# Summing over the second expert table: the high and low inputs pass as one 512-column product

## The chip, the cores and the metric

The kernel runs on one core of a Trainium2 chip. The metric is the device time of one execution, in microseconds: the median of three runs, 2018.12 us, the lowest 2017.0 and the highest 2022.48. In what follows PE is the tensor engine's stream of products, PEld its weight loads, ACT the scalar engine, DVE the vector engine, SP the queue that issues the transfers.

## The reference

The reference is two transformer stages over 256 tokens with 1024 features. The part that the change touches is the expert layer `peer_ffn` of the first stage. Each token scores 16,384 experts by two sets of 128 keys, keeps 16 experts for each of 8 heads, and sums rows of the table `v`, weighted by a gated activation:

```python
def peer_ffn(h, w_q, sub_keys, u, v):
    ...
    def chunk(args):
        hc, ic, gc = args
        a = jnp.einsum('cd,ced->ce', hc, u[ic])
        a = jax.nn.gelu(a, approximate=False) * gc.astype(hc.dtype)
        return jnp.einsum('ce,ced->cd', a, v[ic])
```

Inputs, tables and result are float32.

## The kernel before

The kernel doesn't gather experts. It computes the activation of all 16,384 experts for all 256 tokens, multiplies by the token's weight of each expert (zero for those not chosen), and sums densely over the table `v`. That last sum is the function `expert_sum`: for each of 128 keys j, the 128 experts of that key are the contraction, `arena` holds their weighted activations (128 experts x 256 tokens), and the row block of `v` is 128 experts x 1024 features. The result is 8 feature blocks c of 128 features x 256 tokens, which stay in the accumulation banks over all 128 keys and are added to the residual `x` at the end.

Each float32 operand is split in two of the format fp32r: a high part (rounded) and a low part (what is left). `three` (L509) makes one block product of three: high weights by high input (L512), high weights by low input (L514), low weights by high input (L515). There is one weight load for each product. In `expert_sum` the stationary operand is the table's block and the moving one is the 256 tokens, so a key costs 8 x 3 products of 256 columns.

The work is staged so:

- SP sends one key's 1024 x 128 weights (512 KB) into one of four places of `ring`; a place is free when its low parts are made (`send`, L415).
- ACT makes the high part of half a key's weights, 128 x 512 (`split_high`, L462), once PE has used the half four before it; DVE makes the low part (`split_low`, L468), and PE waits for that before each half. Three halves are prepared ahead (AHEAD). In the same turn of the code ACT makes the high part of a key's input (L2447) and DVE its low part (L2467), two keys ahead.
- A turn of the loop is four keys. The first turn is written out, and 31 more run in a hardware loop. A half is four feature blocks: 12 products of PE, 96 in a turn.
- `next_order` (L517) counts the block products. For most it changes nothing. For a few it hands the 256 columns of one of the three products (L514) in another order: in runs of 16 columns (RUN), taken in turn from each half of the 256 (`parts_at` says 2) or from each quarter (4). The input is read and the bank written in the same order, so the sum is the same. In the loop of this stage it is one of 32 block products per turn; in the written-out first turn it is the fourth, the seventh and the twentieth. Other stages count on in the same way.
- Feature blocks c and c + 1 share a bank of 512 columns, four banks in all, and the first product in a bank clears it.
- After the last half DVE adds the four banks to `x` (L2486), 128 x 512 at a time. The block of code ends there, all engines meet, and the next stage starts: ACT makes the high part of the normed residual (L1059), DVE the low part (L1161), and PE multiplies.

Other places of the program, the wide ones, swap the roles: there 512 columns of weights pass over a stationary 128-token block (the same lines L512, L514, L515, with 128x512 in the form).

Of the kernel before, what the change touches and what calls it, by code (L numbers as in the profile page):

```python
# [23 lines left out]
F32R = mybir.dt.float32r  # L24
BF16 = mybir.dt.bfloat16
ALU = mybir.AluOpType
# [3 lines left out]
P = 128  # L30
T = 256
TT = T // P
D = 1024
DC = D // P
# [6 lines left out]
HALF = 4  # L41
SLOTS = 4
RUN = 16
SIDES = 4
# [11 lines left out]
N_KEYS = 128  # L56
# [241 lines left out]
class Kernel:  # L298
# [1673 lines left out]
    def peer(self):  # L1972

        with self.room(N_KEYS * T):
            with self.pairs(DC):
                self.peer_scores()

            with self.nc.sbuf_tensor("hot", [P, 2, 4, 4, P], F32) as hot:
                self.expert_weights(hot)
            with self.nc.sbuf_tensor("s_high", [P, SIDES, T], F32R) as s_high, \  # L1980
                    self.nc.sbuf_tensor("s_low", [P, SIDES, T], F32R) as s_low:
                self.expert_sum(s_high, s_low)

    def peer_scores(self):

# [407 lines left out]
        for s in (apart, left, right, crossed, merged):  # L2393
            s.total += T // batch

    def expert_sum(self, s_high, s_low):

        nc = self.nc
        first = 2 * (PEER_AT + N_KEYS)
        halves = 2 * RING  # L2400
        turns = N_KEYS // RING
        v = self.dram["peer_v"]
        assert self.split == first + AHEAD
        start = self.sent
        assert start == PEER_AT + N_KEYS + AHEAD // 2 + RING
        cut = self.counter("input_high"), self.counter("input_low")
        with nc.Block(no_gpsimd_drain=True) as block:
            @block.sync
            def _(sp):
                with sp.Fori(0, turns - 2) as it:  # L2410
                    for k in range(RING):
                        g = start + k
                        self.send(sp, g, g % RING, v[it * RING + (g - PEER_AT - N_KEYS)], it, RING)
                self.sent += (turns - 2) * RING
                self.stream(sp, first + 2 * N_KEYS + AHEAD)

            @block.tensor
            def _(pe):
                def turn(it):
                    self.threes = 0 if isinstance(it, int) else 7  # L2420
                    for k in range(RING):
                        pe.wait_ge(cut[1].sem, it * RING + cut[1].at(k + 1))
                        for i in range(2):
                            h = first + 2 * k + i
                            pe.wait_ge(self.low, it * halves + (h + 1))
                            for n in range(HALF):
                                c = HALF * i + n
                                s = slice(n * P, (n + 1) * P)

                                to = self.bank[c // 2][:, (c % 2) * T:(c % 2 + 1) * T]  # L2430
                                opens = isinstance(it, int) and k == 0 and c % 2 == 0
                                ins = self.three(to, ((self.w_high[:, h % SLOTS, s],
                                                       self.w_low[:, h % SLOTS, s]),
                                                      (s_high[:, k % SIDES, :], s_low[:, k % SIDES, :])),
                                                 opens, False, skip_group_check=True)
                            ins.then_inc(self.used, 1)
                turn(0)
                with pe.Fori(1, turns) as it:
                    turn(it)

            @block.scalar
            def _(act):
                def side(k, it):


                    act.wait_ge(self.used, it * halves + (first + 2 * (k - SIDES + 1)))
                    nc.scalar.activation(s_high[:, k % SIDES, :],  # L2447
                                         self.arena[:, bass.ds(it * (RING * T) + k * T, T)],
                                         ACT.Copy).then_inc(cut[0].sem, 1)

                def turn(it, last=False):
                    for k in range(RING):
                        for i in range(2):
                            self.split_high(act, first + AHEAD + 2 * k + i, it, halves)
                        if not last or k < RING - 2:
                            side(k + 2, it)
                side(0, 0)
                side(1, 0)
                with act.Fori(0, turns - 1) as it:
                    turn(it)  # L2460
                turn(turns - 1, True)

            @block.vector
            def _(dve):
                def side(k, it):
                    dve.wait_ge(cut[0].sem, it * RING + cut[0].at(k + 1))
                    nc.vector.tensor_tensor(s_low[:, k % SIDES, :],  # L2467
                                            self.arena[:, bass.ds(it * (RING * T) + k * T, T)],
                                            s_high[:, k % SIDES, :].bitcast(F32), ALU.subtract)\
                        .then_inc(cut[1].sem, 1)  # L2470

                def turn(it, last=False):
                    for k in range(RING):
                        for i in range(2):
                            self.split_low(dve, first + AHEAD + 2 * k + i, it, halves)
                        if not last or k < RING - 2:
                            side(k + 2, it)
                side(0, 0)
                side(1, 0)
                with dve.Fori(0, turns - 1) as it:  # L2480
                    turn(it)
                turn(turns - 1, True)
                dve.wait_ge(self.used, first + 2 * N_KEYS)
                for b in range(DC // 2):
                    part = self.x[:, 2 * b:2 * b + 2, :]
                    nc.vector.tensor_tensor(part, part, self.bank[b][:, :].rearrange(  # L2486
                        "p (c t) -> p c t", c=2), ALU.add)
        for c in cut:
            c.total += N_KEYS
        self.split += 2 * N_KEYS  # L2490
        self.taken += N_KEYS * BLK
# [1037 lines left out]
```

## Time and profile before

| | us |
|---|---|
| median of 3 runs | 2018.12 |
| the profiled execution's own time | 2018.9 |
| its span, first to last instruction | 2017.1 |
| PE busy in the span | 1867.6 (93%) |
| the stage `expert_sum` on PE, first to last product | 829.86 to 1180.41 |
| mean granted clock of PE over the span | 0.975 |

A busy PE says little about its pace, since products overlap: the record of a 256-column product lasts 0.28 us while a new one starts every 0.11 us. The pace is read from the starts of consecutive products. A start is shown to 0.01 us, so the pace is taken over a long run without gaps. The granted clock is 1.00 at 2.4 GHz and 0.50 at 1.2 GHz.

### The profile page before, as it was taken

The page shows a single profiled execution, that of the slowest core. Times are in us where ns is not written, and L with a number is a line of the kernel's source. Part 1 is how long each engine was busy: PE and PEld are TensorE (multiplying, and loading weights), DVE is VectorE, ACT ScalarE, POOL GpSimd, SP SyncE. Part 2 cuts the span into 40 slices and gives each one's busy share as a digit, 9 for nine tenths or more (in the row PEclk, how much of TensorE's full clock was granted, in tenths as well). Part 3 has the DMA queues.
Part 4 walks back from the last instruction along what each step waited for, and adds up shares of the span by engine and source line. Part 5 has one row for each costly group of instructions (what it writes and reads, how often), then busy time and mean ns, then how long its engine had stood idle before and what let it go on. Part 6 is the DMA issues. An engine that isn't in the chain of part 4 may idle for free. (4 is left out here: it accounts for less than half of the span.)

```text
span 2017.1 us, 45016 instructions
## 1 busy us (share of the span) xinstructions
PE 1867.6 (93%) x16518; PEld 1789.4 (89%) x16518; DVE 1454.4 (72%) x3046; ACT 1237.5 (61%) x2420; POOL 0.2 (0%) x4
## 2 busy tenths in 40 slices
PE   8998988999999989999999989687999977899996
PEld 7887888999999976899999989587999976899996
DVE  7667566788986479766666667776787687578857
ACT  5455655777777789655555555733665564666545
POOL 0000000000000000000000000000000000000000
PEclk9999999999999999999999999798999999999998
DMA  6533344466565620266666646101665644166562
GB/s 205 161 98 105 116 146 127 137 196 188 185 184 175 195 83 0 88 194 192 193 192 193 192 141 194 58 3 49 189 197 172 187 136 136 32 185 197 180 194 77
DMA packets 102084, 296.06 MB, mean 147 GB/s; under 512 B 9539, under 2 KB 32454, under 8 KB 101830
## 3 DMA queue, kind: packets, MB, share of 16 engines
q1 hardware_dynamic: 101958, 294.35, 47.5%
q8 instruction: 83, 1.36, 0.3%
q14 instruction: 43, 0.35, 0.1%
HBM read 293.26 MB, written 1.05 MB: 146 GB/s over the span
## 5 line engine op out<-in xcount | busy, mean ns | idle before, releaser
L468 DVE TENSOR_TENSOR w_low<-ring,w_high 128x512 fp32r<-128x512 f32 x1102 | 742.3, 684 | 354.6 <-ACT w_high L462 348.0
L512 PE MATMUL bank<-a_high,w_high 128*128 128x256 f32 x3228 | 917.2, 284 | 78.3 <-DVE w_low L468 42.9
L514 PE MATMUL bank<-a_low,w_high 128*128 128x256 f32 x3228 | 904.8, 280 | 0.0
L515 PE MATMUL bank<-a_high,w_low 128*128 128x256 f32 x3228 | 904.0, 280 | 0.0
L462 ACT ACTIVATE w_high<-ring 128x512 fp32r<-128x512 f32 x1102 | 666.1, 623 | 347.3 <-PE bank L515 345.4
L512 PEld LDWEIGHTS bank<-a_high,w_high 128*128 128x128 f32 x3228 | 616.6, 191 | 95.0 <-DVE w_low L468 44.1
L514 PEld LDWEIGHTS bank<-a_low,w_high 128*128 128x128 f32 x3228 | 616.4, 191 | 0.4
L515 PEld LDWEIGHTS bank<-a_high,w_low 128*128 128x128 f32 x3228 | 616.0, 191 | 0.0
L512 PE MATMUL bank<-s_high,w_high 128*128 128x256 f32 x1024 | 283.6, 277 | 2.0 <-DVE s_low L2467 2.0
L514 PE MATMUL bank<-s_low,w_high 128*128 128x256 f32 x1024 | 283.7, 277 | 0.0
L515 PE MATMUL bank<-s_high,w_low 128*128 128x256 f32 x1024 | 283.6, 277 | 0.0
L512 PEld LDWEIGHTS bank<-s_high,w_high 128*128 128x128 f32 x1024 | 193.1, 189 | 2.2 <-DVE s_low L2467 2.2
L515 PEld LDWEIGHTS bank<-s_high,w_low 128*128 128x128 f32 x1024 | 193.0, 189 | 0.0
L514 PEld LDWEIGHTS bank<-s_low,w_high 128*128 128x128 f32 x1024 | 192.9, 188 | 0.0
L2349 PEld LDWEIGHTS bank<-hot 128*128 128x128 f32 x512 | 61.9, 191 | 29.2 <-issue 18.9
L2093 ACT ACTIVATE arena<-bank 128x256 f32 (+1 forms) x128 | 49.2, 384 | 56.2 <-PE bank L515 55.7
L2349 PE MATMUL bank<-hot 128*128 128x128 f32 x512 | 73.6, 287 | 10.0 <-ACT hot L2286 8.9
L1059 ACT ACTIVATE a_high<-x,params 128x256 fp32r<-128x256 f32 x72 | 32.0, 500 | 49.3 <-DVE x L1292 34.8
L1066 ACT ACTIVATE a_high<-arena 128x256 fp32r<-128x256 f32 x87 | 30.5, 407 | 42.3 <-DVE arena L1352 24.9
L2467 DVE TENSOR_TENSOR s_low<-arena,s_high 128x256 fp32r<-128x256 f32 x128 | 53.4, 418 | 0.8 <-ACT s_high L2447 0.8
L2320 DVE TENSOR_SCALAR hot<-consts,hn 128x128 f32<-128x128 f32 x192 | 53.2, 341 | 0.4 <-PEq L2042 0.4
L2447 ACT ACTIVATE s_high<-arena 128x256 fp32r (+1 forms) x128 | 51.5, 403 | 2.7 <-PEq L2263 2.7
(368 smaller groups left out, 1862.8 us busy)
## 6 DMA issues: line engine op xcount, KB each, us to landing
ring<-in_stream SPq DMA_DIRECT2D x273, 512.0 KB, 3.6
ring<-in_peer_u SPq DMA_DIRECT2D x128, 512.0 KB, 3.6
ring<-in_peer_v SPq DMA_DIRECT2D x128, 512.0 KB, 3.5
ring<-in_stream SPq DMA_DIRECT2D x32, 256.0 KB, 3.2
ring<-in_stream SPq DMA_DIRECT2D x12, 192.0 KB, 2.8
x<-in_x SPq DMA_DIRECT2D x4, 256.0 KB, 6.6
arena<-in_mem SPq DMA_DIRECT2D x1, 1024.0 KB, 11.4
out<-x SPq DMA_DIRECT2D x4, 256.0 KB, 2.6
```

Source lines behind the costliest of these rows:

```text
L462: self.nc.scalar.activation(self.cut(h, self.w_high), self.raw(h), ACT.Copy)\
L468: self.nc.vector.tensor_tensor(self.cut(h, self.w_low), self.raw(h), self.cut(h, self.w_high.bitcast(F32)), ALU.subtract)\
L512: self.nc.tensor.matmul(to, lh, rh, start=start, stop=False, **more)
L514: self.nc.tensor.matmul(order(to), lh, order(rl), start=False, stop=False, **more)
L515: return self.nc.tensor.matmul(to, ll, rh, start=False, stop=stop, **more)
L1059: ins = nc.scalar.activation(self.a_high[:, to, :], source.source[:, c, :], ACT.Copy, scale=self.param(source.gain, c))
L1066: ins = nc.scalar.activation(self.a_high[:, to, :], source[:, c, :], ACT.Copy)
L2093: nc.scalar.activation(to, self.bank[k % 4][:, 0:T], ACT.Gelu)\
L2320: ins = nc.vector.tensor_scalar(hot[:, 1, b, i, :], iota, one(1), one(2), ALU.is_equal, ALU.mult)
L2349: ins = nc.tensor.matmul(self.bank[b][:, i * P:(i + 1) * P], hot[:, 0, b, i, :], hot[:, 1, b, i, :], start=True, stop=True)
L2447: nc.scalar.activation(s_high[:, k % SIDES, :], self.arena[:, bass.ds(it * (RING * T) + k * T, T)], ACT.Copy).then_inc(cut[0].sem, 1)
L2467: nc.vector.tensor_tensor(s_low[:, k % SIDES, :], self.arena[:, bass.ds(it * (RING * T) + k * T, T)], s_high[:, k % SIDES, :].bitcast(F32) ...
```

## The change

In `expert_sum` the high and low part of a key's input now lie side by side in one buffer, `s_both`, with two lots of 256 columns. A block product is two products of PE: the high weights pass over all 512 columns at once (L2431), and the low weights over the 256 columns of the high part (L2435). A feature block then needs a bank of its own: its first 256 columns collect high x high and low x high, its last 256 columns high x low. All eight banks are used. The other order of columns goes to the product of the low weights, one in each turn of the loop as before. At the end DVE adds both halves of each bank to `x`: 16 additions of 128 x 256, in four groups of four, with a wait on its own chain between the two groups that write the same `x`, and a first wait that asks only for the first four feature blocks.

```diff
-            with self.nc.sbuf_tensor("s_high", [P, SIDES, T], F32R) as s_high, \
-                    self.nc.sbuf_tensor("s_low", [P, SIDES, T], F32R) as s_low:
-                self.expert_sum(s_high, s_low)
+            with self.nc.sbuf_tensor("s_both", [P, SIDES, 2, T], F32R) as s_both:
+                self.expert_sum(s_both)
...
+        s_high, s_low = s_both[:, :, 0, :], s_both[:, :, 1, :]
...
-                                to = self.bank[c // 2][:, (c % 2) * T:(c % 2 + 1) * T]
-                                opens = isinstance(it, int) and k == 0 and c % 2 == 0
-                                ins = self.three(to, ((self.w_high[:, h % SLOTS, s],
-                                                       self.w_low[:, h % SLOTS, s]),
-                                                      (s_high[:, k % SIDES, :], s_low[:, k % SIDES, :])),
-                                                 opens, False, skip_group_check=True)
+                                opens = isinstance(it, int) and k == 0
+                                nc.tensor.matmul(self.bank[c][:, :], self.w_high[:, h % SLOTS, s],
+                                                 s_both[:, k % SIDES, :, :], start=opens, stop=False,
+                                                 skip_group_check=True)
+                                order = self.next_order(self.bank[c][:, 0:T])
+                                ins = nc.tensor.matmul(order(self.bank[c][:, 0:T]),
+                                                       self.w_low[:, h % SLOTS, s],
+                                                       order(s_high[:, k % SIDES, :]), start=False,
+                                                       stop=False, skip_group_check=True)
...
-                dve.wait_ge(self.used, first + 2 * N_KEYS)
-                for b in range(DC // 2):
-                    part = self.x[:, 2 * b:2 * b + 2, :]
-                    nc.vector.tensor_tensor(part, part, self.bank[b][:, :].rearrange(
-                        "p (c t) -> p c t", c=2), ALU.add)
+                link = self.chain(dve, "dve")
+                for i in range(2):
+                    dve.wait_ge(self.used, first + 2 * N_KEYS - 1 + i)
+                    for part in range(2):
+                        for c in range(HALF * i, HALF * i + HALF):
+                            ins = nc.vector.tensor_tensor(
+                                self.x[:, c, :], self.x[:, c, :],
+                                self.bank[c][:, part * T:(part + 1) * T], ALU.add)
+                        if part == 0:
+                            link(ins)
```

On PE, the half of the loop's turn that holds the other order of columns stands so before (`128x8x2x16` is that order; banks 2 and 3 hold feature blocks 4 to 7):

```order
L512 MATMUL bank2<-s_high,w_high 128x256
L514 MATMUL bank2<-s_low,w_high 128x8x2x16
L515 MATMUL bank2<-s_high,w_low 128x256
L512 MATMUL bank2<-s_high,w_high 128x256
L514 MATMUL bank2<-s_low,w_high 128x256
L515 MATMUL bank2<-s_high,w_low 128x256
L512 MATMUL bank3<-s_high,w_high 128x256
L514 MATMUL bank3<-s_low,w_high 128x256
L515 MATMUL bank3<-s_high,w_low 128x256
```

The same half on PE with the change:

```order
L2431 MATMUL bank4<-s_both,w_high 128x512
L2435 MATMUL bank4<-s_both,w_low 128x8x2x16
L2431 MATMUL bank5<-s_both,w_high 128x512
L2435 MATMUL bank5<-s_both,w_low 128x256
L2431 MATMUL bank6<-s_both,w_high 128x512
L2435 MATMUL bank6<-s_both,w_low 128x256
L2431 MATMUL bank7<-s_both,w_high 128x512
L2435 MATMUL bank7<-s_both,w_low 128x256
```

Twelve products of 256 columns become four of 512 and four of 256: the columns are the same 3072 in a half, the weight loads are 8 where they were 12.

On DVE, the end of the stage before:

```order
L468 TENSOR_TENSOR w_low<-ring,w_high 128x512 x2
L2467 TENSOR_TENSOR s_low<-arena,s_high 128x256
L468 TENSOR_TENSOR w_low<-ring,w_high 128x512 x2
L2467 TENSOR_TENSOR s_low<-arena,s_high 128x256
L468 TENSOR_TENSOR w_low<-ring,w_high 128x512 x4
L2486 TENSOR_TENSOR x<-x,bank 128x512 x4
```

and with the change:

```order
L468 TENSOR_TENSOR w_low<-ring,w_high 128x512 x2
L2470 TENSOR_TENSOR s_both<-arena,s_both 128x256
L468 TENSOR_TENSOR w_low<-ring,w_high 128x512 x2
L2470 TENSOR_TENSOR s_both<-arena,s_both 128x256
L468 TENSOR_TENSOR w_low<-ring,w_high 128x512 x4
L2491 TENSOR_TENSOR x<-x,bank 128x256 x16
```

The additions stand behind the last low parts of weights in both, and only they differ. On ACT and SP the order of the work is the same as before.

## Rows read from the trace of the kernel before

**Rows 1.** The page: busy time of each engine in the whole span.

```profile
PE 1867.6 (93%) x16518; PEld 1789.4 (89%) x16518; DVE 1454.4 (72%) x3046; ACT 1237.5 (61%) x2420; POOL 0.2 (0%) x4
```

**Rows 2.** Windows of the stage: us, busy us (records) per engine, granted clock, DMA share, GB/s.

```profile
831.00:835.00 4.00, 4.00 (x24) 4.00 (x23) 1.07 (x3) 1.57 (x3) 0.00 (x0) 0.57 0.45 133
840.00:1180.00 340.00, 340.00 (x2997) 340.00 (x2996) 213.99 (x374) 195.79 (x373) 0.00 (x0) 1.00 0.62 193
```

**Rows 3.** Waits between 820 and 1200 us: who waited for whom, us in total, times, longest.

```profile
ACT w_high L462 <- PE bank L515: 153.9, 259, 1.6
DVE w_low L468 <- ACT w_high L462: 131.2, 255, 1.5
PE bank L512 <- DVE a_low L1161: 4.0, 1, 4.0
PE bank L512 <- DVE s_low L2467: 2.0, 1, 2.0
```

**Rows 4.** Timeline of PE in the stage, three places: start us, us, engine, line.

```profile
834.64 0.28 PE L512 MATMUL bank<-s_high,w_high 128*128 128x256 f32 x1
...
838.29 0.28 PE L514 MATMUL bank<-s_low,w_high 128*128 128x256 f32 x1
...
838.88 0.28 PE L512 MATMUL bank<-s_high,w_high 128*128 128x256 f32 x1
...
901.20 0.28 PE L512 MATMUL bank<-s_high,w_high 128*128 128x256 f32 x1
901.32 0.28 PE L514 MATMUL bank<-s_low,w_high 128*128 128x256 f32 x1
...
901.79 0.28 PE L515 MATMUL bank<-s_high,w_low 128*128 128x256 f32 x1
...
902.58 0.28 PE L512 MATMUL bank<-s_high,w_high 128*128 128x256 f32 x1
...
911.76 0.28 PE L512 MATMUL bank<-s_high,w_high 128*128 128x256 f32 x1
```

**Rows 5.** Timeline of PE in a later stage, first and last of 78 products.

```profile
1912.90 0.28 PE L512 MATMUL bank<-a_high,w_high 128*128 128x256 f32 x1
...
1921.97 0.28 PE L515 MATMUL bank<-a_high,w_low 128*128 128x256 f32 x1
```

**Rows 6.** Timeline of PE: 512-column products in fp32r, then 256-column ones.

```profile
1256.92 0.39 PE L514 MATMUL bank<-w_low,a_high 128*128 128x512 f32 x1
...
1263.10 0.39 PE L514 MATMUL bank<-w_low,a_high 128*128 128x512 f32 x1
...
1268.50 0.28 PE L512 MATMUL bank<-a_high,w_high 128*128 128x256 f32 x1
...
1269.20 0.28 PE L512 MATMUL bank<-a_high,w_high 128*128 128x256 f32 x1
```

**Rows 7.** Timeline of PE: two 512-column products in bf16.

```profile
823.81 0.38 PE L2355 MATMUL bank<-hn,small 128*128 128x512 bf16 x1
824.03 0.38 PE L2358 MATMUL bank<-hn 128*128 128x512 bf16 x1
```

**Rows 8.** Timeline of all engines at the end of the stage.

```profile
1180.09 0.69 DVE L468 TENSOR_TENSOR w_low<-ring,w_high 128x512 fp32r<-128x512 f32 x1 [0.67 <-ACT w_high L462]
...
1180.41 0.28 PE L515 MATMUL bank<-s_high,w_low 128*128 128x256 f32 x1
1180.72 2.48 DVE L2486 TENSOR_TENSOR x<-x,bank 128x512 f32<-128x512 f32 x4
1183.55 3.30 ACT L1059 ACTIVATE a_high<-x,params 128x256 fp32r<-128x256 f32 x8 [3.50 <-PEq L2407]
```

**Rows 9.** Timeline of DVE in a later stage: 256-column additions from a bank.

```profile
1343.53 1.40 DVE L2996 TENSOR_TENSOR arena<-arena,bank 128x256 f32<-128x256 f32 x4
```

**Rows 10.** Windows behind the stage, columns as in rows 2.

```profile
1180.00:1182.00 2.00, 0.69 (x7) 0.49 (x5) 1.91 (x4) 0.05 (x1) 0.00 (x0) 1.00 0.76 225
1183.00:1189.00 6.00, 4.28 (x20) 4.31 (x21) 3.48 (x9) 5.45 (x14) 0.00 (x0) 0.50 0.01 3
1190.00:1194.00 4.00, 1.55 (x14) 1.35 (x13) 2.12 (x3) 3.93 (x6) 0.00 (x0) 1.00 0.00 0
```

More of the change, by code:

```diff
@@ L2394, in expert_weights, with expert_sum @@
             s.total += T // batch
-    def expert_sum(self, s_high, s_low):
+    def expert_sum(self, s_both):
+        s_high, s_low = s_both[:, :, 0, :], s_both[:, :, 1, :]
         nc = self.nc
```

## The prediction

> **What bounds the kernel now.** I read the page first: PE is busy 93% of the span, far ahead of DVE (72%) and ACT (61%) [rows 1]. That is an average, so I went to the stage that the change touches. Between 840 and 1180 us PE is busy every microsecond, at the full clock, while DVE works 214 of 340 us, ACT 196, and the transfers take 62% [rows 2]. The waits say the same: ACT waits 153.9 us for PE to give weight slots back, DVE 131.2 us for ACT, and PE waits once for 2.0 us at the stage's start and once for 4.0 us behind its end [rows 3]. So the stage lasts as long as PE's stream of products does, and what counts is the time from the start of one product to the next. That is read from the timeline, not from the busy time.
>
> Three paces of fp32r products can be read there:
> - 256 columns, most of the stage: 81 steps from 902.58 to 911.76, 9.18 us, so 113.3 ns [rows 4].
> - 256 columns, a slower pace: 77 steps from 1912.90 to 1921.97, 9.07 us, so 117.8 ns [rows 5]. The stage itself has it when the full clock comes back: 36 steps from 834.64 to 838.88, 117.8 ns, and 113.3 from there on [rows 4]. The twentieth block product of the first turn, whose middle product has the other order of columns, is the one at 838.29 in between, five steps before 838.88. I read this as two paces of the same stream, with that product as the switch to the faster one.
> - 512 columns: 27 steps from 1256.92 to 1263.10, 6.18 us, so 228.9 ns; the 256-column products right behind such a run go at 6 steps in 0.70 us, 116.7 ns [rows 6].
>
> Two 256-column steps at 113.3 are 226.7, so on these rows the chip charges by the column, and a 512-column product saves nothing over two narrow ones: it costs 2.2 ns more.
>
> **The stream of products.** The stage has 128 keys x 8 feature blocks = 1024 block products. Before, each is 3 x 113.3 = 340.0 ns. With the change it is one of 512 and one of 256 columns, 768 columns as before. No stream that alternates the two widths is in the trace, so I bound it by the rows:
> - both at their seen paces with the narrow one fast: 228.9 + 113.3 = 342.2 ns, +2.2 ns, +2.3 us over 1024.
> - the wide one as good as two fast narrow ones: 226.7 + 113.3 = 340.0, nothing gained.
> - both slow: 228.9 + 117.8 = 346.7, +6.7 ns, +6.9 us.
> - downward, the wide product at the pace of bf16, 0.22 us from one to the next [rows 7]: 220 + 113.3 = 333.3, -6.8 us; and the columns alone at 2.4 GHz: 768 / 2.4 = 320.0, -20.5 us, which no fp32r row comes near.
>
> The wide rows of 228.9 never had the switch of columns in them, so they may be the wide product's slow pace; that speaks for its being a little better here. Nearest are the first two, and I take the middle, +1.2 us, with -7 and +7 as the ends for the range.
>
> On the fixed price of a product the Trainium skill, "TensorE: Matmul & The Clock Gate", section "Back-to-back issue gap", gives N / 2.4 + 2.5 ns between starts at the full clock. By that, one product fewer per block saves 2.5 ns, an estimate of -2.6 us over 1024, which with the additions below would leave +0.6. The trace disagrees: above the columns' own time a narrow fp32r product takes 113.3 - 106.7 = 6.7 ns and a wide one 228.9 - 213.3 = 15.6 [rows 4, 6], an excess that grows with the width instead of standing still.
>
> **The weight loads.** 1024 of 3072 go. They run beside the products, and PE's products leave no gap while PEld is busy as long as PE [rows 2]; I count them at nothing. If they were what sets the 113.3 ns, the narrow product would get cheaper too; that is part of the rival on fixed prices below.
>
> **The preparation of weights and inputs.** It is the same work. A half of PE is 12 x 113.3 = 1.36 us and becomes 1.33 to 1.39. ACT needs 195.79 / 340 and DVE 213.99 / 340 of the time [rows 2], so 0.78 and 0.86 us per half. Both keep their margin at any pace above, as do the transfers at 62%. The high and low input go to other addresses of the same size: nothing. The other order of columns costs 5 steps from 901.20 to 901.79 in 0.59 us where 0.567 would be usual, 0.02 us a turn [rows 4], and is there once a turn before and after.
>
> **The end of the stage.** Here the change adds work on the path. Before, PE's last product starts at 1180.41, DVE's last low part of weights runs from 1180.09 to 1180.78, the four additions take 2.48 us from 1180.72, and ACT starts the next stage at 1183.55 [rows 8]. Nothing else goes on: PE then waits 4.0 us for DVE's first low part [rows 3]. After the change there are 16 additions of 256 columns. Four of them from a bank take 1.40 us [rows 9], so four groups take 5.60. Where a group follows without a wait on the chain it saves a little, and where it waits it loses a little; I take 5.65. That is +3.2 us. The first wait of the change asks only for the first four feature blocks, and could start 8 additions 1.36 us early. It doesn't help, because DVE is at the last low part of weights until 1180.78 anyway, and that stands ahead in its queue; it waited for ACT, which waited for PE's half before the last [rows 8]. Bounds: all 16 without any gap at 0.33 apart, 5.4, so +2.9; each at its full duration of 0.42 and 0.05 at each wait, 6.8, so +4.3. Behind the additions stand the meeting of all engines and the next stage's ACT and DVE work, so the whole of it goes into the time.
>
> **The clock behind the stage.** PE rests from 1180.7 to 1184.7; the clock is 0.50 from 1183 to 1189 while PE works again, and 1.00 by 1190 [rows 10]. A rest of 7.2 instead of 4.0 us meets the same fall; of the 4.3 us of work at half clock none or all could change, which is up to 2.2 us either way. I take 0. The same at the stage's start (0.57 between 831 and 835 [rows 2]), which the change does not move.
>
> **The sum.** +1.2 (stream) + 3.2 (additions) = +4.4 us. The profiled execution took 2018.9 us, of which 2017.1 are the span and 1.8 lie around it: 2023.3 for it. It lies 0.8 us above the median of the runs, 2018.12, so the median would be 2022.5.
>
> **Rivals.**
> 1. *Both widths at the slow pace.* The switch to the fast pace has been seen only in a stream of equal narrow products, and behind a wide one the narrow ones start at 116.7 [rows 6]. If every wide product throws the stream back, the stage is 6.9 us longer; with the additions +10.1: 2028.2. Against it: the fast pace lasts through 340 us of waits, loops and half ends. It decides from a block product above 344 ns.
> 2. *A fixed price per product.* The excess over the columns' time is then paid per product, and 228.9 is only the slow pace of the wide. A fast wide product would cost 213.3 + 6.7 = 220.0; the block product 333.3; -6.8 + 3.2 = -3.6: 2014.5. For it: the narrow stream loses 4.5 ns from fast to slow, and a wide one could lose twice as much, 9, which nearly gives 228.9. It decides below 338 ns. This is the one in which the change makes the kernel faster.
> 3. *More than that.* With a third of the weight loads gone the narrow product also falls towards its columns' 106.7: 216 + 113.3 or 220 + 109 are 329 ns, -11 us, with the additions -8: 2010. Against it: no fp32r row is that fast.
>
> That the change doesn't do what it says would show as PE waiting for weights; with 0.86 of 1.36 us used that needs a mechanism I don't see.
>
> **How the numbers follow.** A measurement of this kernel tells about 0.3%, 6 us, from no change. My forecast case (stream between 0 and +3, additions +3) has 0.46 and gives 2021 to 2024.5; rival 1 has 0.21, rival 2 0.20, rival 3 0.08, and 0.05 is for a clock or wait that I don't see, in either direction. Slower by over 6 us: most of rival 1 and the upper edge of the forecast case, 0.18 + 0.06 + 0.03 = 0.27. Faster by over 6 us: rival 3, the lower part of rival 2 with a clock in its favour, 0.08 + 0.06 + 0.02 = 0.16. The rest, 0.57, is no change to be told. The range from 2013 to 2029 holds the forecast, nearly all of rival 1 and most of rival 2; the forecast case's own range is 2020 to 2025.
>
> **What would show it.** In the profile after: the step from a 512-column product to the next one of the stage, for 24 or more block products. 340 to 342.5 ns is the forecast, 346 and above rival 1, 333 rival 2, under 331 rival 3. Whether the pace changes at the product in the other order of columns, once a turn, tells if the switch still works. The row of L2491 should say 16 additions in 5.4 to 5.9 us, starting right behind the last L468, and PE's wait for L1161 should grow from 4.0 to about 7.2. I am wrong if DVE's additions start well before PE's last product, if PE waits for `w_low` inside the loop, or if the stage's stream is shorter by more than 3 us.

## The result and the profile after

| | before | after |
|---|---|---|
| median, us | 2020.28 (4 runs, 2017.0 to 2022.48) | 2039.14 (4 runs, 2035.62 to 2041.55) |
| profiled execution, us | 2018.9 | 2041.55 |
| span, us | 2017.1 | 2039.8 |
| the stage on PE, first to last product | 350.6 (829.86 to 1180.41) | 363.3 (832.34 to 1195.66) |
| a block product, in the steady stream | 340.0 ns, and 0.02 us more in each turn of 32 | 353.3 ns |
| last additions on DVE | 2.48 | 5.63 |
| PE's wait behind the stage | 4.0 | 7.1 |

The change makes the kernel slower: ratio 1.009, 95% interval 1.0071 to 1.0109, which is 14 to 22 us. The forecast was 2022.5 with a range up to 2029; the time lies outside. It was added to a median of 2018.12, to which a fourth run now adds 2 us; set against each other, the changes themselves are +4.4 forecast and +18.9 measured.

The page after, first the line of busy times, then the two groups of products that replace the three of before and their weight loads (busy us, mean ns of one, idle us before):

```profile
PE 1889.7 (93%) x15494; PEld 1763.3 (86%) x15494; DVE 1458.5 (72%) x3058; ACT 1238.1 (61%) x2420; POOL 0.2 (0%) x4
...
L2431 PE MATMUL bank<-s_both,w_high 128*128 128x512 f32 x1024 | 363.4, 399 | 2.0 <-DVE s_both L2470 2.0
L2435 PE MATMUL bank<-s_both,w_low 128*128 128x256 f32 x1024 | 288.5, 282 | 0.0
L2431 PEld LDWEIGHTS bank<-s_both,w_high 128*128 128x128 f32 x1024 | 193.2, 189 | 49.9 <-DVE s_both L2470 2.2
```

PE has 1024 products fewer than in [rows 1], as meant, and is busy 22 us longer. PEld now has gaps (49.9 us idle). So a third of the weight loads went, they even left room, and nothing came of it. The windows of the stage, with the columns of [rows 2]:

```profile
840.00:1190.00 350.00, 350.00 (x1983) 304.09 (x1982) 213.06 (x372) 195.17 (x372) 0.00 (x0) 1.00 0.60 186
```

PE is without a gap and at the full clock, as before; DVE and ACT do the same work in more time. PE has the bound, and its steps are longer. The timeline of PE in the stage after, the starts of the same product ten blocks apart:

```profile
1000.03 0.40 PE L2431 MATMUL bank<-s_both,w_high 128*128 128x512 f32 x1
1000.26 0.28 PE L2435 MATMUL bank<-s_both,w_low 128*128 128x256 f32 x1
1000.38 0.40 PE L2431 MATMUL bank<-s_both,w_high 128*128 128x512 f32 x1
...
1003.56 0.40 PE L2431 MATMUL bank<-s_both,w_high 128*128 128x512 f32 x1
```

Ten blocks in 3.53 us are 353 ns each. Averaged over 845 to 1190 us, the step after a wide product is 234.9 ns and after a narrow one 118.4. In [rows 4] the narrow step was 113.3. The pace is 353 from the moment the full clock returns (837.0) to the end, and shows no jump at the product in the other order of columns. 13.3 ns x 1024 blocks are 13.6 us; the stage is 12.8 us longer, because the first blocks, at half clock or slow in both, cost the same, and the kernel before pays 0.02 us a turn for its other order.

353.3 ns is also what three narrow products at the slow pace of [rows 5] take, 3 x 117.8 = 353.4. Whether that is more than a coincidence comes up again with the experiments on the width.

The end of the stage after, on DVE, and PE's wait for the next one (waits: who for whom, us, times, longest):

```profile
1195.90 5.63 DVE L2491 TENSOR_TENSOR x<-x,bank 128x256 f32<-128x256 f32 x16
```

```profile
PE bank L512 <- DVE a_low L1161: 7.1, 1, 7.1
ACT a_high L1059 <- PEq L2408: 6.6, 1, 6.6
```

These answer to [rows 8] and [rows 3]: 2.48 us became 5.63, 4.0 became 7.1, and 3.50 became 6.6. The additions start 0.24 us after PE's last product starts, not before it.

The two profiles differ by 22.7 us. Of these, 2.5 are there before the stage begins, in a part of the program that is the same in both; 12.8 are the stage; 3.1 the wait behind it; and 4.3 come later, again in the same program, partly from the clock: after the stage PE works at half clock from 1203.0 to 1209.1, then again from 1212.5 to 1215.9, 9.4 us in all, where before it was 4.8 us from 1184.7. At half clock half of that time is lost, so this is worth about 2.3 us. Of the medians' 18.9 us, the stage and the additions explain 15.9.

### The profile page after: what moved, and what is told of

It is laid out like the page before. It is cut to its first block and busy times, and to the rows that moved or that the text cites. A ratio compares the mean times of both kernels' runs of the same rounds, so it can differ in the third digit from the quotient of the medians.

```text
span 2039.8 us, 42980 instructions
## 1 busy us (share of the span) xinstructions
PE 1889.7 (93%) x15494; PEld 1763.3 (86%) x15494; DVE 1458.5 (72%) x3058; ACT 1238.1 (61%) x2420; POOL 0.2 (0%) x4
## 5 line engine op out<-in xcount | busy, mean ns | idle before, releaser
L2431 PE MATMUL bank<-s_both,w_high 128*128 128x512 f32 x1024 | 363.4, 399 | 2.0 <-DVE s_both L2470 2.0
L2435 PE MATMUL bank<-s_both,w_low 128*128 128x256 f32 x1024 | 288.5, 282 | 0.0
L2431 PEld LDWEIGHTS bank<-s_both,w_high 128*128 128x128 f32 x1024 | 193.2, 189 | 49.9 <-DVE s_both L2470 2.2
L2435 PEld LDWEIGHTS bank<-s_both,w_low 128*128 128x128 f32 x1024 | 192.9, 188 | 0.0
L2470 DVE TENSOR_TENSOR s_both<-arena,s_both 128x256 fp32r<-128x256 f32 x128 | 53.6, 419 | 0.8 <-ACT s_both L2450 0.8
L2450 ACT ACTIVATE s_both<-arena 128x256 fp32r (+1 forms) x128 | 51.7, 405 | 2.7 <-PEq L2262 2.7
L1667 DVE CUSTOM_DVE_ANT_0 arena<-bank,arena 128x256 f32<-128x256 f32 (+1 forms) x48 | 19.2, 402 | 39.3 <-PE bank L1612 39.0
L1612 PE MATMUL bank<-arena 64*128 64x128 f32 (+4 forms) x144 | 41.5, 376 | 5.7 <-DVE arena L1302 4.1
```

The lines of the kernel that those rows point to most:

```text
L2431: nc.tensor.matmul(self.bank[c][:, :], self.w_high[:, h % SLOTS, s], s_both[:, k % SIDES, :, :], start=opens, stop=False, skip_group_check ...
L2435: ins = nc.tensor.matmul(order(self.bank[c][:, 0:T]), self.w_low[:, h % SLOTS, s], order(s_high[:, k % SIDES, :]), start=False, stop=False ...
L2450: nc.scalar.activation(s_high[:, k % SIDES, :], self.arena[:, bass.ds(it * (RING * T) + k * T, T)], ACT.Copy).then_inc(cut[0].sem, 1)
L2470: nc.vector.tensor_tensor(s_low[:, k % SIDES, :], self.arena[:, bass.ds(it * (RING * T) + k * T, T)], s_high[:, k % SIDES, :].bitcast(F32) ...
```

## The experiments

All ran beside the kernel before. The pace is read from one window, 900 to 1100 us, in the middle of the stage: all records of the stage are there, so 200 us over the count of PE's products is the mean step. The count takes in the records that run across the window's edges, two or so, which makes the step 0.1 to 0.2% too short; the starts themselves give 113.3 for the fast narrow pace, 117.8 for the slow one and 233.3 for a stream of wide products.

**First: is it the order of columns, the width, or the banks?**

The kernel before with all products in the usual order:

```diff
-                                ins = self.three(to, ...)
+                                order = self.next_order(to)
+                                high, low = self.w_high[:, h % SLOTS, s], self.w_low[:, h % SLOTS, s]
+                                nc.tensor.matmul(to, high, s_high[:, k % SIDES, :], ...)
+                                nc.tensor.matmul((to), high, (s_low[:, k % SIDES, :]), ...)
+                                ins = nc.tensor.matmul((to), low, (s_high[:, k % SIDES, :]), ...)
```

> The kernel before, with all products of the stage in the usual order of columns: three narrow products a block, no product in the other order. Theory S (the stream has a fast and a slow pace, and a product in the other order is what brings the fast one; in the changed kernel it fails to): the block product takes 3 x 117.8 = 353 ns, the stage about 363 us instead of 350.7, the whole +12 to +13 us against before. Theory W (alternating widths is what costs, the order of columns is not what sets the pace): 340 ns, stage 350 us, whole time as before.

Measured: ratio to before 1.0027 (1.0005 to 1.0049). The ten times scatter more than before's nineteen (2015.2 to 2025.7): six lie between 2020.1 and 2023.1, and four at 2026.9, 2029.8, 2034.5 and 2035.3. The profiled one, of 2026.9, has the fast pace all through the stage, but for 3.4 us at half clock near its start; the stage lasts 349.8 us:

```profile
900.00:1100.00 200.00, 200.00 (x1767) 200.00 (x1766) 126.27 (x221) 115.68 (x221) 0.00 (x0) 1.00 0.62 192
```

200 / 1767 is 113.2 ns. The fast pace came without the other order of columns. So S is wrong in its strong form: that order is not needed for it. The same kernel once more:

> A second look at the narrow products in the usual order of columns. Its ten times lay between 2020 and 2035, and the profiled one had the pace of 340 ns. If the pace is a matter of chance without the other order of columns, the profiles and times of this kernel fall in two groups, some 13 us apart (353 or 340 ns a block); if not, its stage shows 340 ns again and the scatter comes from elsewhere.

Measured: one time of 2030.6, and this time the profile shows the slow pace, from the first product to the last; the stage lasts 361.8 us:

```profile
900.00:1100.00 200.00, 200.00 (x1701) 200.00 (x1700) 121.97 (x213) 111.27 (x213) 0.00 (x0) 1.00 0.61 185
```

200 / 1701 is 117.6 ns (117.8 by the starts), three of them 353. The same kernel has a stage of 350 or of 362 us. In these two profiles the narrow stream without the other order keeps the pace it begins with, 12 us apart over the stage; the whole times don't fall in two clean groups, since the rest of the program scatters by some us.

The two profiles differ in one more thing. With the fast pace the granted clock falls to 0.50 from 835.9 to 839.3 us; with the slow one it stays at 1.00 from before the stage to its end. The clock may have a part in this, for in the kernel before the pace changed over such a stretch. These are its first products, nine steps in 1.02 us:

```profile
830.08 0.28 PE L514 MATMUL bank<-s_low,w_high 128*128 128x256 f32 x1
...
831.10 0.37 PE L514 MATMUL bank<-s_low,w_high 128*128 128x256 f32 x1
```

That is 113.3 ns. The clock is at 0.50 from 831.15 to 834.56, and behind it the pace is 117.8 [rows 4], until the product in the other order. In the three other narrow kernels profiled with such a stretch the fast pace came back behind it. What picks the pace is thus not shown: neither the clock nor the order of columns accounts for all of these profiles.

The changed kernel without the other order:

```diff
-                                ins = nc.tensor.matmul(order(self.bank[c][:, 0:T]),
+                                ins = nc.tensor.matmul(self.bank[c][:, 0:T],
                                                        self.w_low[:, h % SLOTS, s],
-                                                       order(s_high[:, k % SIDES, :]), start=False,
+                                                       s_high[:, k % SIDES, :], start=False,
```

> The changed kernel without the other order of columns. S: nothing is lost, since it had no effect: block product 353 ns, stage 363.4 us, whole time as the changed kernel (+18 us against before). W: the same 353 ns. If the other order did something there, this is slower than 353 ns, or faster where it only cost.

Measured: 1.0097 (1.0074 to 1.012), stage 363.3 us, 353 ns a block. As the changed kernel: the other order on the low-weight product does nothing there, good or bad.

The changed kernel with the other order on the wide product:

```diff
-                                nc.tensor.matmul(self.bank[c][:, :], self.w_high[:, h % SLOTS, s],
-                                                 s_both[:, k % SIDES, :, :], start=opens, ...)
-                                order = self.next_order(self.bank[c][:, 0:T])
+                                order = self.next_order(self.bank[c][:, 0:T])
+                                nc.tensor.matmul(order(self.bank[c][:, :]), self.w_high[:, h % SLOTS, s],
+                                                 order(s_both[:, k % SIDES, :, :].rearrange(
+                                                     "p u t -> p (u t)")), start=opens, ...)
...
+                                ins = nc.tensor.matmul(self.bank[c][:, 0:T], ...)
```

> The changed kernel with the other order of columns on the 512-column product instead of the low-weight one, at the same places (runs of 16 taken in turn from the high and the low half, or from quarters). S: the switch works on the product that fills most of the stream: 340 to 343 ns a block, stage 350 to 352 us, whole time +3 to +6 us against before. W: still 353 ns, +18 us.

Measured: 1.0089 (1.0059 to 1.0119), stage 363.3 us:

```profile
900.00:1100.00 200.00, 200.00 (x1134) 173.84 (x1133) 121.96 (x213) 111.29 (x213) 0.00 (x0) 1.00 0.59 185
```

1134 products are 567 blocks, 353 ns. S expected 340 to 343 and fails; the switch does not work on a wide product either.

Banks and additions of the change, with narrow products:

```diff
-                                nc.tensor.matmul(self.bank[c][:, :], self.w_high[:, h % SLOTS, s],
-                                                 s_both[:, k % SIDES, :, :], start=opens, ...)
...
-                                ins = nc.tensor.matmul(order(self.bank[c][:, 0:T]), ...)
+                                high, low = ...
+                                nc.tensor.matmul(self.bank[c][:, 0:T], high, s_high[:, k % SIDES, :], start=opens, ...)
+                                nc.tensor.matmul(order(self.bank[c][:, T:2 * T]), high, order(s_low[:, k % SIDES, :]), ...)
+                                ins = nc.tensor.matmul(self.bank[c][:, 0:T], low, s_high[:, k % SIDES, :], ...)
```

> The changed kernel's buffers, banks and last additions, with three narrow products a block as before and the other order on the middle one: high x low goes to the second half of the bank. S: 340 ns a block, stage 350.7 us, and only the additions remain: +3 to +4 us against before. A third theory, B (the cost comes from eight banks in turn, or from the place in the bank, not from width or order): 353 ns here too, +16 to +18 us.

Measured: 1.0023 (1.0007 to 1.0039), that is +1.4 to +8 us. The stage lasts 350.4 us, the additions 5.62, PE's wait behind it 7.2:

```profile
900.00:1100.00 200.00, 200.00 (x1764) 200.00 (x1762) 125.98 (x220) 115.35 (x221) 0.00 (x0) 1.00 0.61 193
```

```profile
1182.47 5.62 DVE L2491 TENSOR_TENSOR x<-x,bank 128x256 f32<-128x256 f32 x16
```

Theory B falls: eight banks, the side-by-side buffer and the second half of the bank cost PE nothing. What is left is the additions. The rest of the loss, over 12 us, comes with the wide product, that is with its width and the weight load that it spares; the two can't be had apart here.

**Second: what about the width?**

Low weights over all 512 columns too:

```diff
-                                ins = nc.tensor.matmul(order(self.bank[c][:, 0:T]),
+                                ins = nc.tensor.matmul(self.bank[c][:, :],
                                                        self.w_low[:, h % SLOTS, s],
-                                                       order(s_high[:, k % SIDES, :]), start=False,
+                                                       s_both[:, k % SIDES, :, :], start=False,
```

> The changed kernel with the low weights passed over all 512 columns too, so that the stream has one width (it adds the product low x low, which the others leave out). No other order of columns. Theory W (alternating the widths costs): 2 x 229 = 458 ns a block, the pace of the wide places, stage about 471 us. Rival P (a 512-column product over this input is slow by itself, whatever stands beside it): 2 x 235.6 = 471 ns, stage about 484 us. The whole kernel is 105 to 125 us slower than the changed one, for its 262,144 more columns.

Measured: 2156.7 us (2 runs), ratio 1.067 (1.0648 to 1.0691), stage 479.3 us:

```profile
900.00:1100.00 200.00, 200.00 (x859) 160.29 (x858) 92.17 (x161) 84.23 (x161) 0.00 (x0) 1.00 0.45 139
```

200 / 859 is 232.8 ns a wide product (233.3 by the starts from 845 to 1300 us), between W's 229 and P's 235.6, which is two slow narrow steps. Neither is right alone. In a stream of one width the wide product costs 6.6 ns more than two fast narrow ones, 226.7. With a fast narrow one beside it that would be 346.6 ns a block; the changed kernel takes 353.3. With a slow narrow one (117.8) it would be 351.1, still too little.

Wide products of a half first, then the narrow ones:

```diff
                                 nc.tensor.matmul(self.bank[c][:, :], self.w_high[:, h % SLOTS, s],
                                                  s_both[:, k % SIDES, :, :], start=opens, ...)
+                            for n in range(HALF):
+                                c = HALF * i + n
+                                s = slice(n * P, (n + 1) * P)
                                 order = self.next_order(self.bank[c][:, 0:T])
```

> The changed kernel with the four wide products of a half first, and then its four narrow ones: the width changes twice in eight products instead of eight times. W: the excess falls with the number of changes, so between 340 and 346 ns a block, stage 351 to 357 us, +5 to +11 us against before. P: 353 ns, nothing changes, +18 us.

Measured: 1.0063 (1.0046 to 1.008), stage 357.0 us. The timeline of PE, merged, with the start and length of each group of four:

```profile
1000.10 1.09 PE L2431 MATMUL bank<-s_both,w_high 128*128 128x512 f32 x4
1001.03 0.62 PE L2438 MATMUL bank<-s_both,w_low 128*128 128x256 f32 x4
1001.49 1.09 PE L2431 MATMUL bank<-s_both,w_high 128*128 128x512 f32 x4
1002.42 0.62 PE L2438 MATMUL bank<-s_both,w_low 128*128 128x256 f32 x4
1002.88 1.09 PE L2431 MATMUL bank<-s_both,w_high 128*128 128x512 f32 x4
```

Four wide take 0.93 us, four narrow 0.46: 1.39 us for four blocks, 347 ns each. The same products, weights and banks in another sequence are 6.3 us faster in the stage than one after the other, so P, which expected no difference, falls, and about half of the 13.3 ns a block depends on the sequence. W foresaw the direction and not the size: 347 ns lies just outside its 340 to 346, and +9 to +16 us largely above its +5 to +11.

The starts tell where the half comes from. Over the turns of the loop, the steps behind the four narrow products are 118.4, 114.5, 113.6 and 113.4 ns: the first is as slow as every narrow step in the changed kernel, and by the third the stream is back near its fast pace. Behind the four wide ones they are 225.8, 235.9, 230.8 and 235.9. So a wide product doesn't throw the stream into the slow pace for good; its neighbour pays. The other half, 7 ns, is near the 6.6 by which a product in the all-wide stream exceeds two fast narrow ones. That the loss is the sum of these two is an inference from two different streams, and that 353.3 equals three slow narrow steps stays unexplained.

The low-weight product added to the other half of the bank:

```diff
-                                ins = nc.tensor.matmul(order(self.bank[c][:, 0:T]),
+                                ins = nc.tensor.matmul(order(self.bank[c][:, T:2 * T]),
```

> The changed kernel with the low-weight product added to the second 256 columns of the bank, where high x low is collected (the sum at the end is the same). A fourth theory, A: what costs is that the narrow product returns to the columns at which the wide one began, or does so too soon or too late; then the pace moves away from 353 ns, most likely to 340-347. W and P: 353 ns a block, +18 us against before.

Measured: 1.0104 (1.0087 to 1.0121), stage 363.3 us, 353 ns. A falls.

**Third: does moving the other order matter, and has the wide stream two paces?**

The other order of columns on the low-weight product of the narrow kernel:

```diff
-                                ins = self.three(to, ...)
+                                order = self.next_order(to)
...
+                                nc.tensor.matmul(to, high, s_high[:, k % SIDES, :], ...)
+                                nc.tensor.matmul((to), high, (s_low[:, k % SIDES, :]), ...)
+                                ins = nc.tensor.matmul(order(to), low, order(s_high[:, k % SIDES, :]), ...)
```

> The kernel before with the other order of columns on the low-weight product instead of the middle one, at the same places: the one part of the change that moves it, done alone. Theory W2 (the narrow stream holds a fast or slow pace, any product in the other order brings the fast one; with wide products among them there is no fast pace to bring): 340 ns a block, stage 350.6 us, whole time as before and no time above 2027. Rival L (on the low-weight product it doesn't work, and that is part of the loss): the pace is left to chance as in the kernel without it, 340 or 353 ns, times up to 2035.

Measured: 0.9997 (0.9984 to 1.0009), ten times from 2015.5 to 2025.8, stage 350.4 us with the fast pace, 113.4 ns:

```profile
900.00:1100.00 200.00, 200.00 (x1764) 200.00 (x1763) 126.01 (x221) 115.49 (x221) 0.00 (x0) 1.00 0.62 193
```

No difference, and none of the ten times above 2027. L falls: which of the products carries the other order doesn't matter. That it protects from the slow pace rests on little: this kernel and the one before have no time above 2026.5, and the one without it has four of eleven above 2029; but the narrow kernel with the new banks, which has it and 3 us of additions more, has one time of 2032.7 of ten.

The all-wide kernel with the other order on the high-weight product:

```diff
-                                nc.tensor.matmul(self.bank[c][:, :], self.w_high[:, h % SLOTS, s],
-                                                 s_both[:, k % SIDES, :, :], start=opens, ...)
+                                order = self.next_order(self.bank[c][:, 0:T])
+                                nc.tensor.matmul(order(self.bank[c][:, :]), self.w_high[:, h % SLOTS, s],
+                                                 order(s_both[:, k % SIDES, :, :].rearrange(
+                                                     "p u t -> p (u t)")), start=opens, ...)
...
+                                ins = nc.tensor.matmul(self.bank[c][:, :], ...)
```

> The kernel with all products of the stage at 512 columns (it adds low x low), with the other order of columns on the high-weight product at the places of the change. Without it the block took 466.4 ns, 233.2 a product. W2: no fast pace for wide products, 466 ns and a stage of 479 us again. Rival F (the wide stream has a fast pace too, and 233.2 is its slow one): 2 x 226.7 to 2 x 229, 453 to 458 ns, stage 466 to 471 us, 8 to 13 us less than without.

Measured: 2156.0 us (2 runs), stage 479.4 us, the same 859 products in 200 us. No second pace for wide products was found this way.

## Why the prediction was wrong

- *The bound, right.* The stage lasts as long as PE's stream; ACT, DVE and the transfers had the margin that was worked out, and PE waited for no weights in the loop.
- *The stream of products, wrong: this is the failed step.* It was put at +1.2 us with +6.9 as the upper end ("both slow: 228.9 + 117.8 = 346.7"), and measured +12.8 over the stage. Two things were wrong in it. The pace of 228.9 ns was taken from places where weights pass over stationary tokens, and I treated it as the wide product's slow pace, if anything an upper bound ("that speaks for its being a little better here"). Over this input it is 233.3 in a stream of its own and 234.9 beside narrow products. And the bound for a mixed stream was the sum of paces read in unmixed ones; the changed kernel takes 6.7 ns a block more than that sum with the fast narrow pace (353.3 against 233.3 + 113.3 = 346.6), and 2.2 more than with the slow one. Nothing in the profile bounded a mixed stream from above, and the text said that no such stream was there, and then used the nearest rows as an end.
- *Rival 1 had the right direction and place.* With a wide product before each of them the narrow steps are 118.4 ns, near the 117.8 it used. But it was priced at 6.9 us, by the wrong wide pace; with 233.3 its sum is 351.1 ns, 11.4 us. And its picture, a stream thrown back to the slow pace, holds only product by product: four narrow ones in a row come back to 113.4.
- *The switch, half right.* That two paces exist, 113.3 and 117.8, and that the stream can stay in one is what the two profiles of the narrow kernel without the other order show, 350 against 362 us. That a product in the other order is what brings the fast one in the unchanged kernel fits its timeline, but the fast pace also comes without it. With wide products in the stream it brought no faster pace at any of the three places tried: the low-weight product, the wide one, and the all-wide stream.
- *Rivals 2 and 3, wrong.* There is no gain from fewer products or fewer weight loads: PEld got 49.9 us of idle time and the steps became longer. The formula that the prediction took from the Trainium skill, "TensorE: Matmul & The Clock Gate", section "Back-to-back issue gap", N / 2.4 + 2.5 ns, would by the prediction's estimate have made the stage 2.6 us shorter; the section gives it for a product by itself, not for a stream of weight loads and products. The trace disagrees, the stage became 12.8 us longer.
- *The additions, right.* Forecast 5.65 us and +3.2; measured 5.63, and PE's wait went from 4.0 to 7.1. The queue behind the last low part of weights took away the early start, as worked out. With the new banks and additions but narrow products, the kernel loses 1.4 to 8 us.
- *The clock, put at nothing, at the edge of its bounds.* PE works 9.4 us at half clock behind the stage where it worked 4.8 before, about 2.3 us of time, against bounds of 2.2 either way. The change need not be the cause: the narrow kernel without the other order, whose last additions and 4.0 us wait are those of before, works 9.2 us at half clock there in its first profile.

Open: why a 512-column fp32r product costs more than two of 256 here, why alternation adds to it, and what makes the two paces. For the loss with wide products the experiments excluded the banks, the place in the bank and the order of columns. That the wide places of the program run at 229 and this stream at 233.3 was not followed up. No tried version beats the kernel before; the nearest with wide products, grouped, is 0.6% slower.

## What to carry to other kernels

Before fewer and wider products are written, read the step from start to start in streams of the same mix and the same operands. The sum of paces from unmixed streams was no upper bound here: 346.6 or 351.1 ns against 353.3. A wide output that must be folded at the end has a price that can be worked out beforehand: twice the additions, on the path, behind whatever is queued on that engine.

## What was not expected of the hardware

- A gapless stream of 256-column fp32r products, each with its own weights, runs at 113.3 or at 117.8 ns a product at the same granted clock of 1.00, and can keep either to the end of a stage of 3072: 349.8 and 361.8 us for the same kernel, the first with 3.4 us at half clock in it.
- A 512-column product takes 233.3 ns in a stream of its own over the same input, and 234.9 in turn with 256-column ones, which then take 118.4; four and four in turn take 232 and 115 in the mean, and of the four narrow steps only the first is slow (118.4, the last 113.4).
- A 256-column product whose columns go in runs of 16, taken in turn from both halves, costs about 0.02 us more than one in the usual order.
